# Second attention of a two-block kernel: keys on partitions from the first product, instead of probabilities turned on TensorE

## The reference

```python
# A: banded. 8 query heads, 2 key heads, 64 wide, blocks of 128 queries
scores = where(|q_pos - k_pos| <= 128 or key is context, q k^T * 64 ** -0.5, -inf)
m = max(max(scores), sink)                     # one sink per head
e = exp(scores - m);  o_a = (e / (sum(e) + exp(sink - m))) @ v_a
# B: not banded, no sink; q and k are normalised per head
o_b = softmax(q k_all^T * 64 ** -0.5) @ v_all  # 512 tokens + 256 context = 768 keys
y = (g_a * (o_a @ w_branch_a) + g_b * (o_b @ w_branch_b)) @ w_out
```

## Time and profile before

| what | us |
|---|---|
| median of 3 runs | 1759.01 (1758.84 to 1761.44) |
| the profiled execution, its own time | 1752.29 |
| its span in the profile | 1750.5 |
| granted TensorE clock, mean | 0.998 of full speed |
| busy: TensorE matmul | 1711.7 |
| busy: VectorE, ScalarE, GpSimd | 970.0, 668.4, 838.1 |

### The profile page before, as it was taken

How to read it: one execution, slowest core, us unless ns; L and a number is a source line. 1 busy time by engine, 2 the same in 40 slices (tenths; PEclk the granted TensorE clock), 3 DMA queues, 4 the chain that set the end, 5 groups by cost and what they waited for, 6 DMA issues and landing times.

```text
span 1750.5 us, 25522 instructions
## 1 busy us (share of the span) xinstructions
PE 1711.7 (98%) x8591; PEld 1419.0 (81%) x8591; DVE 970.0 (55%) x1637; ACT 668.4 (38%) x1407; POOL 838.1 (48%) x677
## 2 busy tenths in 40 slices
PE   8999999999999999999999999989999999999997
PEld 6888888888877888888888888767778988888887
DVE  4258645767885467252124439387668674542544
ACT  5322222243466422223223223666632732332333
POOL 4554454567971545544544545301144665544541
PEclk9999999999999999999999999999999999999999
DMA  7454452534211446533333333001022234323321
GB/s 225 117 172 153 145 157 84 174 97 127 73 49 53 129 132 192 156 87 103 118 87 93 108 97 96 13 1 49 25 61 85 58 102 142 96 85 108 96 84 49
DMA packets 279971, 178.46 MB, mean 102 GB/s; under 512 B 6536, under 2 KB 258628, under 8 KB 279748
## 3 DMA queue, kind: packets, MB, share of 16 engines
q1 hardware_dynamic: 265620, 149.36, 29.4%
q10 hardware_dynamic: 14256, 27.87, 4.6%
HBM read 175.11 MB, written 2.10 MB: 101 GB/s over the span
## 4 chain that ended last, share of the span: by engine, by line
PE 90%; DVE 6%; issue 1%; ACT 1%; DMA 1%; POOL 0%; DVEq 0%; ACTq 0%; POOLq 0%
PE ps L844 86%; PE ps L1325 3%; DVE mod_acc L2075 2%; DVE prob2A L2344 1%; DVE acc L2030 0%; DVE actL L2149 0%; PE ps L1150 0%; ACT actH L1655 0%; DVE x L2146 0%; DMA mod_raw<-in_w_mod 0%; POOL wL L724 0%; PE ps L1458 0%; DVE x L2118 0%; DVE probT2A L2394 0%; DMA const<-in_const 0%
## 5 line engine op out<-in xcount | busy, mean ns | idle before, releaser
L724 POOL TENSOR_TENSOR wL<-raw,wH 128x512 fp32r<-128x512 f32 (+2 forms) x560 | 747.7, 1359 | 712.9 <-ACT wH L1570 701.2
L844 PE MATMUL ps<-actH,wH 128*128 128x512 f32 (+1 forms) x1312 | 510.7, 389 | 4.4 <-POOL actL L778 1.9
L844 PE MATMUL ps<-actH,wL 128*128 128x512 f32 (+1 forms) x1312 | 503.6, 384 | 0.0
L844 PE MATMUL ps<-actL,wH 128*128 128x512 f32 (+1 forms) x1248 | 479.6, 384 | 0.0
L1570 ACT ACTIVATE wH<-raw 128x512 fp32r<-128x512 f32 (+2 forms) x558 | 311.4, 608 | 327.6 <-PE ps L844 327.6
L844 PEld LDWEIGHTS ps<-actH,wH 128*128 128x128 f32 x1312 | 247.1, 188 | 55.7 <-ACT wH L1601 2.3
L844 PEld LDWEIGHTS ps<-actH,wL 128*128 128x128 f32 x1312 | 246.4, 188 | 49.1
L844 PEld LDWEIGHTS ps<-actL,wH 128*128 128x128 f32 x1248 | 235.2, 188 | 46.4 <-issue 0.7
L844 PE MATMUL ps<-hidH,wH 128*128 128x512 f32 (+1 forms) x720 | 267.6, 372 | 0.0
L844 PE MATMUL ps<-hidH,wL 128*128 128x512 f32 (+1 forms) x720 | 266.6, 370 | 0.0
L844 PE MATMUL ps<-hidL,wH 128*128 128x512 f32 (+1 forms) x720 | 266.5, 370 | 0.0
(11 more groups left out here) (357 smaller groups left out, 1996.5 us busy)
## 6 DMA issues: line engine op xcount, KB each, us to landing
mod_raw<-in_w_mod ACTq DMA_DIRECT2D x24, 1024.0 KB, 6.3
raw<-in_w_in SPq DMA_DIRECT2D x48, 512.0 KB, 3.7
raw<-in_ffn_w_up SPq DMA_DIRECT2D x44, 512.0 KB, 3.8
raw<-in_w_up SPq DMA_DIRECT2D x44, 512.0 KB, 3.8
raw<-in_ffn_w_gate SPq DMA_DIRECT2D x43, 512.0 KB, 3.8
raw<-in_ffn_w_down SPq DMA_DIRECT2D x32, 512.0 KB, 4.1
raw<-in_w_out SPq DMA_DIRECT2D x16, 512.0 KB, 4.0
raw<-in_w_down SPq DMA_DIRECT2D x16, 512.0 KB, 4.0
```

The source lines that it names most:

```text
L724: nc.gpsimd.tensor_tensor(wL[:, b:b + w // 2], raw[:, b:b + w // 2], wH[:, b:b + w // 2].bitcast(F32), ALU.subtract).then_inc(lo_ready, 1)
L844: return nc.tensor.matmul(out, a, b, start=first, stop=last)
```

## The change

The logits are computed twice. A first set, as before with queries on partitions, serves only to find each row's maximum (with the sink, in the banded branch); for the unbanded branch it is made from the high part of the keys alone, and of the banded branch's low part only the rows that hold it are used. VectorE takes the maxima (`maximum`), eight per tile of queries, one tile ahead. From them comes a shift per query and head, four columns at a time, which TensorE turns into four rows (`shift_rows`) and VectorE lays out beside the queries (`shift_spread`).

The second set is made with the keys on partitions: a block of 128 keys stationary, four heads by 128 queries moving, 512 columns (`turned_logits`). One matmul has the high part of the keys; the second has the low part, and its operands carry the shift in four more rows, so that the maximum is subtracted in the product. Masked blocks get the mask by a third matmul. ScalarE's exponential then gives probabilities that already have the keys on partitions (`turned_probs`), and they are the moving operand of the values (`step_values`). There is one step for each block of keys: 4 or 5 for a banded tile, 6 for an unbanded one, 42 in all; each handles both key heads, in one PSUM bank each (banks 4 and 5).

The row sums are sums over partitions now: the probabilities of all steps are added elementwise, by GpSimd (`add_probs`; the last step of unbanded tiles by VectorE, `last_add`), on top of a diagonal with the sink's term in the banded branch, and one product with a block of ones gives the sum on every partition (`totals_spread`). VectorE inverts that, 512 columns, and multiplies (`normalise2`). The values are copied out of PSUM first, by ScalarE.

Seven of the eleven turns, and the first set of logits of tile 0, are made within the last gate slabs; the Exp of ScalarE's table comes before two of the gates. Two halves of the first merge slabs are multiplied within the last tile's steps. Some queries lie in the weight slots, so that the merge's third and fourth slab are loaded after tile 3's totals, and its fifth after tile 5.

The diff, cut to its core:

```diff
-    TURN_AT = {3: 5, 6: 6, 9: 7, 12: 8, 16: 9, 20: 10}
+    TURN_AT = {(0, 0): 7, (0, 1): 8, (1, 0): 9, (1, 2): 10}
...
+    STEPS2 = [(T, s) for T in range(TILES2) for s in range(len(key_blocks(T)))]
...
+    EARLY_TURNS = {(0, 1): (0, 1, 2, 3), (1, 1): (4,), (1, 6): (5,), (2, 5): (6,)}
+    EARLY_LOGITS = {(1, 3): 0, (1, 5): 1, (1, 7): 2, (2, 1): 3, (2, 3): 4, (2, 4): 5, (2, 6): 6, (2, 7): 7, (3, 7): NH}
+    EARLY_ROWS = {(3, 1): 0, (3, 5): 1}
+    AHEAD = ([[1, 2], [3, 4], [5, 6], [7]], [[], [0, 1, 2], [3, 4, 5], [6], [7]], [[0], [1, 2, 3], [4, 5], [6], [7]],
+             [[0], [1, 2, 3], [4, 5], [6, 7, 8]], [[1], [2, 3], [4], [5, 6], [7], [8]], [[1], [2, 3], [4], [5, 6], [7], [8]],
+             [[1], [2, 3], [4], [5, 6], [7], []], 6 * [[]])
+    VALUES_AT = {4: {2: (0, 1)}, 5: {2: (0, 1)}, 6: {2: (0, 1), 4: (2, 3)}}
+    LAST_VALUES = {4: (2, 3), 5: (2, 3, 4), 6: (4, 5)}
+    TOTAL_AT = (0, 1, 1, 2, 2, 2, 2, 2)
...
# gpsimd
+        def add_probs(T, e, kv):
...
+            before = prob2(T, 0, kv) if wide(T) and e == first else total
+            G.tensor_tensor(total[:], before[:], prob2(T, e, kv)[:], ALU.add).then_inc(added_p, 1)
...
# tensor
+        def logits2(n):
...
+            else:
+                pe.wait_ge(lg_max, n - 1)
...
+                if wide(T):
+                    mm = product(out, own, kHB[:, key:key + w], True, True)
+                else:
+                    product(out, own, kHA[:, key:key + w], True, False)
+                    mm = product(out, own[lower], kLA[lower, key:key + w], False, True)
...
+        def turned_logits(T, e, kv):
...
+                pe.wait_ge(prob_ready, 2 * i - 1 + kv)
...
+            product(out, kH[:, a:a + P], queries(T, kv), True, False)
+            mm = product(bank(4 + kv), kL[rows, a:a + P], shifted_q[T % 2 * 2 + kv][rows, :], False, m is None)
+            if m is not None:
+                mm = product(out, maskR[:, m * P:(m + 1) * P], identR[:].unsqueeze(1).broadcast_to([P, 4, P]), False, True)
...
+        def step_values(T, e):
...
+            for kv, half in enumerate((lower, upper)):
+                mm = product(ps[half, 7, :], v[:, b * NKV * DH + kv * DH:][:, 0:DH], prob2(T, e, kv)[:],
+                             e == 0, e == last_step(T))
...
+        def totals_spread(T):
...
+            for kv, half in enumerate((lower, upper)):
+                mm = product(ps[half, 6, :], unit[:], total2(T, kv)[:], True, True)
...
         def second_attention():
-            for u in range(len(group2)):
...
+            for T, e in STEPS2:
+                soon = ahead(T, e)
+                turned_logits(T, e, 0)
+                if e == last_step(T) and T + 1 < TILES2:
+                    shift_rows(T + 1, 0)
+                if e > 0:
+                    for n in soon[:1]:
+                        logits2(n)
+                elif T > 0:
+                    shift_rows(T, 1)
+                    for before in LAST_VALUES[last_step(T - 1) + 1]:
+                        step_values(T - 1, before)
+                turned_logits(T, e, 1)
+                for n in soon[:1] if e == 0 else ():
+                    logits2(n)
+                for n in soon[1:2]:
+                    logits2(n)
+                if e > 0:
+                    if T > 0 and e == TOTAL_AT[T]:
+                        totals_spread(T - 1)
+                    for before in VALUES_AT[last_step(T) + 1].get(e, ()):
+                        step_values(T, before)
+                if (T, e) in TURN_AT:
+                    turn2(TURN_AT[T, e])
+                for n in soon[2:]:
+                    logits2(n)
+                if T == TILES2 - 1 and e in (1, 3):
+                    merge_part(e // 2, range(4))
...
# scalar
+        def turned_probs(T, e, kv):
...
+            nc.scalar.activation(prob2(T, e, kv)[:], bank(4 + kv), ACT.Exp, scale=DH ** -0.5).then_inc(prob_ready, 1)
...
# vector
+        def maximum(n):
...
+            if wide(T):
+                V.tensor_reduce(into, room, AX_X, ALU.max).then_inc(lg_max, 1)
...
+        def normalise2(T):
...
+            V.reciprocal(sums, sums).then_inc(inverted, 1)
...
+            V.tensor_tensor(into, into, sums, ALU.mult).then_inc(attn_out, 1)
...
+                for n in ahead(T, e):
+                    maximum(n)
+                if T > 0 and e == TOTAL_AT[T]:
+                    normalise2(T - 1)
```

More of the change, by code:

```diff
@@ L440, in units1 @@
                            out=attn1[:, tile * ATT:(tile + 1) * ATT], sink=False)
[L442 to L456, removed]
-                else:
-                    blocks, pieces, mask = ([tile + 1, tile + 2, tile + 3, 0, 1], [(latents[tile], 384), (context, 256)],
-                                            cv("band")[:, 0:5 * P])
-                    first += P
-                products, at_col = [], first
-                own = (qA0[:, head * P:(head + 1) * P] if banded and tile == 0 else
-                       q[:, head * S + tile * P:][:, 0:P])
-                for key, w in pieces:
-                    products.append((at_col, [(own, kH[:, key:key + w]), (own, kL[:, key:key + w])]))
-                    at_col += w
-                yield dict(W=P * len(blocks), products=products, col0=first, mask=mask,
-                           v=[v[:, b * NKV * DH + kv * DH:][:, 0:DH] for b in blocks], head=head, sink=banded)
@@ L1862, in second_attention @@
[L1862 to L1863 removed]
+                for kv in range(NKV):
+                    turned_probs(T, e, kv)
+                if (T, e) in TURN_AT:
+                    for branch in range(2):
+                        turned_high(TURN_AT[T, e], branch)
+                if e in (1, 2) and T + 1 < TILES2:
+                    queries_copied(T + 1, e - 1)
+                if e == last_step(T) and T + 1 < ST:
+                    sink_term(T + 1, 0)
@@ new lines, in maximum @@
+        def maximum(n):
+            T, head = divmod(n, NH)
+            at_col, pieces, mask = room_of(n)
+            room = flat[:, at_col:at_col + sum(w for _, w in pieces)]
+            into = stat[:, n % 16:n % 16 + 1]
+            dve.wait_ge(lg_done, n + 1)
+            if wide(T):
+                V.tensor_reduce(into, room, AX_X, ALU.max).then_inc(lg_max, 1)
+            else:
+                V.tensor_tensor_reduce(out=room, in0=room, in1=mask, scale=-(DH ** -0.5), scalar=sink[:, NH + head:][:, 0:1],
+                                       op0=ALU.add, op1=ALU.min, accum_out=into).then_inc(lg_max, 1)
+            if head % 4 == 3:
+                shift(T, head // 4)
```

534 lines of the change are left out of this document (332 added, 202 removed).

## The result

The kernel with the change takes **1776.97 us** (median of 4 runs, 1769.68 to 1785.55); the kernel before, beside it, 1758.99 (1758.84 to 1761.44). The ratio is 1.0101, 95% interval 1.0055 to 1.0147: slower by 18 us, where the forecast was 13 us faster, and outside its range of 1730 to 1757.

What follows compares the result with a forecast made beforehand. TensorE's own work and its waits between matmuls of the second attention were taken as the bound; 7.6 us less work plus 5.2 us less waiting saved 13 us from 1759.0, giving 1746 us, range 1730 to 1757.

Steps and rivals of the forecast that it cites:

- The forecast's stretch: From the last four gate slabs to the merge's second round: 184 us forecast instead of 197.
- banded first logits: TensorE's logits for the banded maxima, low half on 64 rows, priced by columns alone: 16.5 us.
- turned logits: TensorE's second logits, keys on partitions: 168 matmuls of 512 columns at 0.227 us, 38.1 us.
- values and totals: TensorE's value products, 0.85 us a step, 35.8 us in all, and totals over partitions, 6.8 us.
- waits: TensorE's waits in the second attention, counted by queue order: 18.4 us against 23.6 before.
- rival D: Value halves with 512 moving columns no longer run side by side, 43 us more: 1789 us, chance 0.02.
- The reciprocal: VectorE's inversion over 512 columns, once in each of eight tiles: 3.6 us from its slope, ends 0.69 and 5.2.
- Rival A: VectorE's reciprocal streams in 0.69 us, so 14 us of the waits go: 1732 us, chance 0.17.
- C: Slower, VectorE is the bound: gain gone at a 5.2 us reciprocal, 1775 us at twice the slope; chance 0.10.
- Costs taken as nothing: GpSimd's adds, 2.7 us per step, costed at nothing; ScalarE's exponentials hidden behind TensorE with 0.2 us to spare.
- Rival B: Hand-offs aren't better: TensorE still loses 23 us and only the work is saved: 1751 us, chance 0.16.
- The sum against the median: The 13 us saved were taken off the median 1759.0 us, 6.7 above the profiled execution, giving 1746.

Runs made afterwards that it cites:

- c4: The kernel with the change, its two middle banded tiles issuing their four logit products high, high, low, low instead of high, low, high, low; 1769.0 us.
- a1: The kernel with the change, with the low product of the banded logits on all 128 rows instead of 64, added rows zero; 1762.4 us.
- b1: The kernel with the change without the banded logits' low product, its reciprocal now in four pieces between four maxima and its product later; 1767.3 us.
- a3: The kernel with the change, with the reciprocal replaced by a multiplication by one, only to price it; 1762.5 us.
- a4: The kernel with the change, without the banded logits' low product and with the reciprocal replaced by a multiplication by one; 1741.3 us.
- c3: The kernel with the change, without banded low products, last totals before the merge's third slab, reciprocal in earlier-placed pieces, no early exponential in the gates; 1746.3 us.
- b2: The kernel with the change without banded low products, with sums by eight one-column products, a reciprocal of 8 columns and eight spreading products; 1765.2 us.

## Why the prediction was wrong

The forecast's stretch was 43.6 + 122.2 + 18.4 = 184.2 us; measured 214.5. By start times in the profile of after:

| term | forecast | measured | difference |
|---|---|---|---|
| banded first logits | 16.5 | 39.2 | +22.7 |
| turned logits, 0.235 each, not 0.227 | 38.1 | 39.5 | +1.4 |
| the same, behind a 64-row product | 0 | 1.3 | +1.3 |
| values and totals | 42.6 | 46.4 | +3.8 |
| half clock, two pieces | 0 | 3.4 | +3.4 |
| waits (what is left) | 18.4 | 16.1 | -2.3 |

- **The step that failed** is "Banded heads keep it on 64 rows, columns being what costs: 16 by 4 by 0.115 and 16 by 2 by (0.17 + 0.115) = 16.5". Columns are what costs as long as the number of rows of the weights stays the same. Each step between 128 and 64 rows takes 0.2 us more (c4); 128 of them in the stretch cost 22.7 us, and 1.3 in the product behind. With the step priced as measured the sum of the forecast is 11 us slower (24.0 less 13) instead of 13 faster. The trace of before has products on 64 rows only in plain float32, in pairs, in the first attention, and none between fp32r products of 128 rows; that should have made this an unknown with bounds on both sides. It was given one value, and no rival rested on it. Why a change of rows costs this is not shown; the records show only that the weight load no longer runs ahead.
 The Trainium skill bears on this (TensorE: Matmul & The Clock Gate, Part 3: Packing small matmuls — row/col tiling, What overlaps and what doesn't): it says that loads of weights overlap running matmuls only where the row groups differ. The trace doesn't agree here: in a1 products that all use 128 rows follow each other every 0.115 us, each load starting with the product before (1156.46 for the product at 1156.63), and it is where the row counts differ that the load starts only with its own product (1164.43).
- **Values and totals** were scaled by columns from the earlier trace rows. Inside a group of steps a step does take 0.85 us, but each group loses some 0.15 at its edges, which makes 0.93 per step. A size was off, the halves did run side by side: rival D (1789 us) falls.
- **The clock** had no term. Inside the stretch it cost 3.4 us in the profiled execution; over the runs, 0.987 to 0.996 where the kernel before has a median of 0.994 to 0.995. The clock is lowest, 0.988, where TensorE waits longest (b1), and of the changed kernels highest, 0.995, in the two without an inverse.
- **The reciprocal** was forecast at 3.6 us by its slope and measured at 3.356: the steps on it hold. Rival A (it streams) falls, and so does C, in which it passes 5.2 us (half as much again as 3.6 would be 5.4). The kernel ended on C's side of no change through another mechanism. The estimate from the Trainium skill (VectorE: DVE Perf Modes, First, the fixed hardware budget, for the eight repeats, and Specifications for the clock) was 4.4 us; a column costs (3356 - 200) / 504 = 6.3 ns by the rows of 512 and of 8 columns, where eight repeats at 0.96 GHz would be 8.3. The measurement decides.
- **The waits** came out at 16.1 us against 18.4, but partly for the wrong reason: the three waits forecast in tiles 0 to 2 (1, 3 and 1.5) didn't show, because TensorE was busy with its slow logits. a1 shows them as soon as those are quick, 4.1 us on TensorE and 7.8 on its weight loads. Tiles 4 to 6 take 18.1 us on average where 16.5 was forecast with a wait of 1.5 in it: that wait was right (1.2 to 1.9 us by a3), the rest of the tile, 16.5 in a3, was put at 15. At the end 1.2 us for the last exponentials and 3.7 for the low part were forecast: TensorE doesn't stop before the last values (1289.75), and the hole for the low part is 3.3.
- **Costs taken as nothing** held. GpSimd's adds at 1273 ns are named by TensorE's weight loads for 0.6 us in all, exponentials at 596 ns (forecast 0.69) for 0.4 on its matmuls and 7.3 on its weight loads, in 17 pieces of at most 0.8; how much of that TensorE would have waited anyway is not shown. Rival B (only the work is saved) stands on waits of 23 us; they were 16.
- **The sum against the median**: profiled and median run were taken to lie 6.7 us apart; it was 7.3. That this held is luck, as the forecast gave no reason for it and the four runs lie 16 us apart.

What the scheme can be worth is read from a4 and c3. Without the banded low products and without a reciprocal it runs at 1741.3 us, 15 under the kernel before; with the inverse, better placed, and the two edits beside it, at 1746.3, 10 under it. Two details, the low products (most of it their 64 rows) and the reciprocal, cost it 35.7 us. A kernel with the low products on 128 rows and the reciprocal well placed was not run.

## What to carry to other kernels

A smaller tile of the array isn't free because its columns are few: before taking a product from 128 to 64 rows, look at its neighbours, and where they use 128, keep 128 with zeros or group the products of equal rows. Where VectorE's longest instruction has grown, count not its time but what stands behind it in the queue and which bank its result frees: in pieces and a step earlier it cost 5.5 us less by the median (2.8 by the ratios), in pieces and later 9 more (4.6). And look at time multiplied by granted clock beside the medians, since kernels that differ in their holes differ in the clock too.

## What the runs showed of the hardware that was not expected

- A change of the weights' rows between 128 and 64 costs 0.2 us (0.31 from start to start for 256 columns instead of 0.115). A change between 128 and 68 costs nothing: 0.24 us for 512 columns in the same rows. Why 68 is free and 64 isn't was not tried. At a change the record of the weight load starts with its own product and no longer with the one before. The first fp32r product behind plain float32 work shows the same in after: load and product start together at 1244.32, and the next product follows 0.34 us later, as behind 64 rows.
- The reciprocal takes 0.205 us for 8 columns, 0.936 for 128 and 3.356 for 512.
- VectorE's operation on four columns (L2609) has a mean of 0.727 us, with single ones from 0.169 to 2.532, where the earlier trace rows show 0.158 and 0.200 us for two and eight columns of another operation. In b2 it is 0.592. Its cause wasn't tested.
- A hole of 3.3 us was followed, 0.2 to 0.6 us behind its end, by 3.4 us at half clock (1.2 GHz) in three profiles of five; with matmuls in the hole, in one profile, nothing came behind it. Behind a hole of 2.2 us it was six profiles of seven, in four of them only after 1.1 to 1.6 us, and behind the three of 2.1 to 2.4 us in the kernel before it never was. What decides is open. Four executions of one kernel differ by 16 us, and multiplied by their clocks by 3.5.
